# First mixer: the output gate's four projection tiles leave the middle of the attention loop; two stand at its end, two in the recurrence's first two chunks

## What is computed

```python
def even_mixer(h, w_in, w_out, sinks, conv_w, conv_b, i_bias, f_bias, ml_norm):
    p = h @ w_in
    q_a, k_a, v_a, qk_m, v_m, o_m, i_m, f_m = split_cols(p, ...)
    ...
    y_att = sliding_window_sink_attention(q, k, v, sinks)        # 8 query heads of 64, window 128
    ...
    hm = mlstm_chunkwise(q_m, k_m, v_m, log_i, log_f)            # 4 heads, 4 chunks of 128 tokens
    hm = head_layernorm(hm, ML_NORM_EPS).reshape(bsz, T, ML_V_W) * ml_norm.astype(F32)
    y_ml = (hm * jax.nn.sigmoid(o_m.astype(F32))).astype(h.dtype)
    return jnp.concatenate([y_att, y_ml], axis=-1) @ w_out
```

## Time and profile before

| | |
|---|---|
| device time, median of 3 runs | 1441.8 us (1441.53 to 1442.5) |
| the profiled execution | 1446.55 us |
| its span | 1444.7 us |
| PE busy | 1355.6 us, 94% of the span |
| DVE, ACT, POOL busy | 587.0, 541.5, 653.6 us (41%, 37%, 45%) |
| matmuls of tiles (24 a tile), mean of one | 400 to 410 ns, overlapping |
| granted PE clock, mean over the span | 0.961 |

### The profile page before, as it was taken

The page is one execution under the profiler, slowest core; times in us unless marked ns, Lnnn a source line. Parts: engine busy times, 40 slices in busy tenths (PEclk is TensorE's granted clock), DMA queues, the critical chain, the costliest instruction groups (busy, mean ns, idle before and its releaser), DMA issues.

```text
span 1444.7 us, 17744 instructions
## 1 busy us (share of the span) xinstructions
PE 1355.6 (94%) x6427; PEld 1089.8 (75%) x6427; DVE 587.0 (41%) x966; ACT 541.5 (37%) x883; POOL 653.6 (45%) x801
## 2 busy tenths in 40 slices
PE   5999967999999999999899997998799999999998
PEld 4777646788888888886578776888678888888886
DVE  4537575421211212345599376355442122121233
ACT  4346643441322323337444425332334132241332
POOL 5653213564555645553345321211265555455562
PEclk9999978999999999999799988999999999999999
DMA  8322101323323333232122210000033233332321
GB/s 268 88 76 65 50 1 29 103 88 93 98 88 100 89 97 92 87 102 59 44 73 73 59 59 15 1 2 1 29 92 98 88 96 94 89 100 87 102 88 59
DMA packets 202131, 109.13 MB, mean 76 GB/s; under 512 B 4570, under 2 KB 199376, under 8 KB 201936
## 3 DMA queue, kind: packets, MB, share of 16 engines
q1 hardware_dynamic: 201648, 108.16, 25.8%
q0 software_dynamic: 416, 0.07, 0.0%
HBM read 106.11 MB, written 2.10 MB: 75 GB/s over the span
## 4 chain that ended last, share of the span: by engine, by line
PE 75%; DVE 6%; ACT 3%; issue 2%; POOL 0%; DVEq 0%; ACTq 0%; POOLq 0%
PE ps L825 21%; PE ps L826 21%; PE ps L827 21%; PE ps L812 2%; PE ps L1192 1%; DVE late L2397 1%; PE ps L1206 1%; PE ps L1119 1%; PE ps L1245 1%; PE ps L1217 1%; PE ps L1080 0%; PE ps L1260 0%; PE ps L1258 0%; PE ps L1235 0%; ACT arena L1582 0%
## 5 line engine op out<-in xcount | busy, mean ns | idle before, releaser
L747 POOL TENSOR_TENSOR w_lo<-raw_w,w_hi 128x256 fp32r<-128x256 f32 x760 | 618.2, 845 | 639.3 <-ACT w_hi L1311 639.3
L1311 ACT ACTIVATE w_hi<-raw_w 128x1024 fp32r<-128x1024 f32 x190 | 201.2, 1059 | 594.5 <-PE ps L827 447.7
L825 PE MATMUL ps<-hn_hi,w_hi 128*128 128x512 f32 x880 | 360.8, 410 | 3.4 <-POOL w_lo L747 2.5
L826 PE MATMUL ps<-hn_lo,w_hi 128*128 128x512 f32 x880 | 352.8, 401 | 0.0
L827 PE MATMUL ps<-hn_hi,w_lo 128*128 128x512 f32 x880 | 352.4, 400 | 0.0
L825 PE MATMUL ps<-hid_hi,w_hi 128*128 128x512 f32 x640 | 254.2, 397 | 1.1 <-DVE hid_lo L1795 1.1
L826 PE MATMUL ps<-hid_lo,w_hi 128*128 128x512 f32 x640 | 253.8, 397 | 0.0
L827 PE MATMUL ps<-hid_hi,w_lo 128*128 128x512 f32 x640 | 253.7, 396 | 0.0
L825 PEld LDWEIGHTS ps<-hn_hi,w_hi 128*128 128x128 f32 x880 | 168.4, 191 | 53.4 <-issue 11.3
L826 PEld LDWEIGHTS ps<-hn_lo,w_hi 128*128 128x128 f32 x880 | 168.4, 191 | 42.4 <-issue 3.1
L827 PEld LDWEIGHTS ps<-hn_hi,w_lo 128*128 128x128 f32 x880 | 168.2, 191 | 41.2
(11 more groups left out here) (363 smaller groups left out, 1339.4 us busy)
## 6 DMA issues: line engine op xcount, KB each, us to landing
raw_w<-in_w_up SPq DMA_DIRECT2D x64, 512.0 KB, 4.0
raw_w<-in_w_down SPq DMA_DIRECT2D x64, 512.0 KB, 3.6
raw_w<-in_o_w_in SPq DMA_DIRECT2D x27, 512.0 KB, 3.8
raw_w<-in_e_w_in SPq DMA_DIRECT2D x19, 512.0 KB, 3.7
raw_w<-in_e_w_out SPq DMA_DIRECT2D x8, 512.0 KB, 4.0
raw_w<-in_o_w_out SPq DMA_DIRECT2D x8, 512.0 KB, 3.5
rwkv_raw<-in_x SPq DMA_DIRECT2D x4, 512.0 KB, 8.3
out<-arena SPq DMA_DIRECT2D x8, 256.0 KB, 2.9
```

The lines of the kernel that those rows point to most:

```text
L747: nc.gpsimd.tensor_tensor(w_lo[:, n % CUT, ks], raw_w[:, n % RING, ks], w_hi[:, n % CUT, ks].bitcast(F32), ALU.subtract).then_inc(w_cut, 1)
L825: mm(o, a_hi, b_hi, start=(k == 0), stop=False)
L826: mm(o, a_hi, b_lo, start=False, stop=False)
L1311: A(w_hi[:, n % CUT], raw_w[:, n % RING], ACT.Copy).then_inc(w_high, 1)
```

## The change

It replaces the rule "tile 11+u in step u" by two tables. Steps 0 to 3 keep the v tiles; steps 4, 5 and 6 have none; o0 stands in step 7 and o1 in step 9; o2 and o3 stand in chunks 0 and 1, between the scores and the local state, and are turned one chunk later. ACT drains o2 and o3 there, into a new buffer, and takes the Sigmoid at the start of chunk 2, between the roots, so one more table is loaded. `w_ml` gets other places in memory.

```diff
+SLOT_BESIDE = {0: 11, 1: 12, 2: 13, 3: 14, 7: 15, 9: 16}
+SLOT_IN_CHUNK = {0: 17, 1: 18}
...
     for u in range(8 + 3):
-        if u < 8:
-            yield "slot", 11 + u
+        if u in SLOT_BESIDE:
+            yield "slot", SLOT_BESIDE[u]
         if u == 0:
             yield "rope", 3
-        if 1 <= u < 9:
-            yield "turn", EVEN_SLOTS[10 + u][1][1:]
+        if u - 1 in SLOT_BESIDE:
+            yield "turn", EVEN_SLOTS[SLOT_BESIDE[u - 1]][1][1:]
...
+        o_tile = cut(y_t, 2048, 2, T)
...
-        w_ml = cut(late, 0, 4, 4, P)
+        w_ml = [cut(relu_t.rearrange("p a t -> p (a t)"), n * 512, 4, P) for n in range(2)]
+        w_ml += [cut(arena, 2048 + n * 512, 4, P) for n in range(2)]
...
                         close(ins, "qk_st", n, par)
+                    if n in SLOT_IN_CHUNK:
+                        project_in(0, SLOT_IN_CHUNK[n])
+                    if n - 1 in SLOT_IN_CHUNK:
+                        key = EVEN_SLOTS[SLOT_IN_CHUNK[n - 1]][1]
+                        drained(pe, *key)
+                        turn(key[1:], [o_tile[:, n - 1, t * P:(t + 1) * P] for t in range(NT)])
...
-            for j in range(4):
-                drained(act, "o", j)
-            A(o_gate, o_gate, ACT.Sigmoid).then_inc(S["o_sig"], 1)
...
             for n in range(NT):
+                if n in SLOT_IN_CHUNK:
+                    drain(o_tile[:, n, :], *EVEN_SLOTS[SLOT_IN_CHUNK[n]][1])
+                    cut_next()
+                if n - 1 in SLOT_IN_CHUNK:
+                    drain_gate(EVEN_SLOTS[SLOT_IN_CHUNK[n - 1]][1][1:])
+                if n == 2:
+                    for j in range(4):
+                        drained(act, "o", j)
+                    A(o_gate, o_gate, ACT.Sigmoid).then_inc(S["o_sig"], 1)
                 for a in range(2):
```

More of the change, by code:

```diff
@@ L1512, in _ @@
                     for j in range(4):
-                        ins = A(w_ml[:, u, j, :], mtmp[:, u % 2, j * P:(j + 1) * P], ACT.Exp, bias=gg[:, u, j:j + 1])
+                        ins = A(w_ml[u][:, j, :], mtmp[:, u % 2, j * P:(j + 1) * P], ACT.Exp, bias=gg[:, u, j:j + 1])
                     ins.then_inc(S["n_keep"], 1)
@@ L2054, in ml_out @@
                     j = 4 * n + hh
-                    ins = V.tensor_scalar(w_ml[:, n, hh, :], w_ml[:, n, hh, :], mv[:, j, 0:1], mv[:, j, 1:2],
+                    ins = V.tensor_scalar(w_ml[n][:, hh, :], w_ml[n][:, hh, :], mv[:, j, 0:1], mv[:, j, 1:2],
                                           ALU.subtract, ALU.mult)
@@ L2124, in ml_combine @@
                 for hh in range(4):
-                    ins = V.tensor_scalar(w_ml[:, n, hh, :], nn[:, hh // 2, hh % 2, 0:P], dn[:, n % 2, hh:hh + 1], None,
+                    ins = V.tensor_scalar(w_ml[n][:, hh, :], nn[:, hh // 2, hh % 2, 0:P], dn[:, n % 2, hh:hh + 1], None,
                                           ALU.mult)
@@ L2129, in ml_combine @@
                 for hh in range(4):
-                    ins = V.bn_stats(st6[:, hh, :], w_ml[:, n, hh, :])
+                    ins = V.bn_stats(st6[:, hh, :], w_ml[n][:, hh, :])
                 link(ins)
```

12 lines of the change are left out of this document (9 added, 3 removed).

## The result

| | before | changed |
|---|---|---|
| median of 7 runs | 1442.5 us | 1453.06 us |
| lowest, highest | 1441.53, 1448.77 | 1444.53, 1454.32 |
| ratio, 95% interval | | 1.0043 [1.0023, 1.0062] |
| profiled execution, span | 1446.55, 1444.7 | 1452.59, 1450.8 |
| transposes of k | 184.07 | 180.16 |

The changed kernel is slower: 0.43%, some 6.2 us (3.3 to 8.9). The medians lie further apart than the ratio says, 10.6 us, since both kernels' times spread over 7 us or more. The sign is clear of the noise in both; the size is known only to lie between 3.3 and 12.6.

A forecast was written before the change was run, and what follows sets the result against it. PE bounds the kernel as a whole and the attention loop, DVE the recurrence. -5.5 + 4.4 + 3.7 + 1.7 = +4.3 on 1441.8 gives 1446.1 us; range 1440.4 to 1449.4, the forecast's own 1443.7 to 1448.3.

The forecast's parts named there:

- Term 1: Attention loop: two tiles and turns leave PE, new waits for DVE's probabilities take part back; it ends 5.55 earlier, -5.5 us.
- term 4: Attention loop: PE's clock falls to 1.2 GHz after the second new wait, at 148.5; +1.7 us (0 to 2.6).
- first wait: Attention loop: PE newly waits some 3 us for the probabilities of step 3.
- second wait: Attention loop: PE newly waits some 3.4 us for the probabilities of step 4, until 148.48.
- Term 2: Entry of the recurrence, transposes of k to first combine: 19.0 us with two tiles instead of 14.62, +4.4 us.
- Term 3: Rest of the recurrence: POOL's gain (2.8) and low parts (0.9) delay DVE's instructions; +3.7 us (0 to 6.8).
- The rule of the Trainium skill: DVE instructions with two SBUF inputs, or in a two-port mode, and GpSimd block each other fully; term 3 up to 6.8.
- rival (d): Recurrence: meetings with DVE cost whole POOL instructions; +7.4 us, 1449.2 us, chance 10%.
- (a): Entry of the recurrence: tiles vanish in its waits, hidden under DVE's time; 1436.3 us, chance 8%.
- (b): Recurrence: POOL's instructions miss DVE's; 1440.7 us with the clock staying, 1442.4 with its fall, chance 12%.
- (c): Attention loop: the clock does not fall, POOL's meetings as forecast; +2.6 us, 1444.4 us, chance 20%.
- Costed at nothing: ACT's extra table load (1.28) and drains, the weights' DMAs and w_ml's new places: no cost; 3.2 if ACT's cover went.

The follow-up runs named there:

- e2: Changed kernel with POOL's low part of the output projection's second tile moved behind the gate's multiplications; ratio 1.0059 to the kernel before.
- e3: Changed kernel with the loop's two gate tiles in steps 4 and 6 instead of 7 and 9; ratio 1.0006 to the kernel before.
- e4_one: Changed kernel with one gate tile in the recurrence (chunk 0) instead of two, the others in steps 4, 5 and 8; ratio 0.9976 to the kernel before.
- e1: Changed kernel without POOL's four multiplications of the gate by the norm's gain, signals kept; ratio 1.0026 to the kernel before.
- e6: Changed kernel with all gate tiles back in steps 4 to 7; late Sigmoid, late gain and weights' places stay; ratio 1.0034 to the kernel before.
- e12: e4_one with Sigmoid and gain split by gate tile, POOL's last two multiplications waiting for places where DVE reads PSUM; ratio 0.9951 to the kernel before.
- e5: e4_one with Sigmoid and gain split by gate tile, three POOL multiplications ahead of the low part, one behind; ratio 0.9976 to the kernel before.

## Why the prediction was right

The forecast was +4.3 us and slower. Measured were +6.2 (3.3 to 8.9) and, with the same kernel again, +9.4 (6.2 to 12.6), which is above the +7.6 where the forecast's range ended; the median of the changed kernel, 1453.06, is above that range too (it ended at 1449.4). At the transposes of y_ml, where all its terms end, it was +4.16 in the first pair of traces and +3.51 in the second. So the sum held up to there, and what it left out is what lies behind. Term by term, in the first pair:

- **Term 1, the loop, -5.5, and term 4, the clock, +1.7:** together -3.8, measured -3.9 (184.07 to 180.16). The first wait was 2.86 (3.0 forecast). The second was 1.80, where the prediction says 3.4 and its own times give 4.1 (from 140.14, with turns and output 2.65, a row 0.46 and a score 1.14, to 148.48). It was shorter since PE came to it later (its transposes and outputs behind the first wait took 1.54 and 3.17 at the low clock instead of 1.09 and 1.88) and DVE was half a microsecond ahead of my sum; the slip doesn't enter the term, which goes by DVE's times. The first gate tile ended at 157.22 (157.60 forecast). The fall that counts was not where I put it, behind the second wait, but behind the third, 2.22 us long, which I had inside the 6.10 us from step 7's score to the next probabilities and not named as a wait. Its price, 1.73, shows in e2's trace, where it did not happen; I had 1.7. The first fall cost nothing, as the next wait took it up. So the size of term 4 came true by luck: its reason, that a wait longer than the earlier ones of 1.78 and 2.79 brings a fall, doesn't hold in these traces. A wait of 2.22 brought one in three traces out of four, and one of 3.30 in e3 brought none.
- **Term 2, the entry, +4.4:** measured 18.46 - 14.62 = +3.8. The sum of PE's work held (19.0 forecast); local state and numerator took 1.05 and 1.06 at the full clock, where I had put 1.26 from a row at a mixed one. e4_one adds what the sum implied and I had not drawn from it: one tile would have been free.
- **Term 3, POOL beside DVE, +3.7:** measured 31.95 - 27.72 = +4.2, of which 1.2 in the first combine (0.9 forecast) and 3.0 in the second (2.8). e2 shows the first and e1 and e6 the second. The mechanism and the count of the second combine were right, the equal size of 0.70 by luck: four POOL instructions met three short instructions and L2151, which took 0.22, 1.02, 1.03 and 0.74 more. In the first combine the low part met three instructions, not two, for 0.23, 0.48 and 0.49 more. In these rows each stretched instruction of DVE starts while one of POOL's runs and ends within 0.05 us of its end (the first of L2151's four within 0.1), and as DVE's instructions depend on each other, each is caught by the next of POOL's.
- **The rule of the Trainium skill** ("SBUF — State Buffer", "Who interferes with whom") agrees with the traces: 1.19 us for an instruction of 0.17 that ends with POOL's of 1.27 is blocking, not sharing; the two of 1.19 in the changed kernel have both inputs in SBUF; and e12's instruction at 198.68, with one of its inputs in PSUM, and the reciprocal, with a single one, were not slowed. Two inputs in SBUF are not the whole of it: the TENSOR_SCALAR instructions, with one data input in SBUF, were slowed as well (L2145 0.17 to 1.05 in e4, L2118 1.18 to 3.47 in e5). That would be the other case of this page of the Trainium skill, a two-port mode; no view here names the mode. The upper case, rival (d), +7.4, did not come: of POOL's 4.95 us, 0.9 lay before the second combine, and the rest also covers the time that DVE's instructions take by themselves.
- **The rivals.** (a), the tiles vanish in the waits, is refuted for two tiles and true for one (e4_one). (b), POOL misses, by the rows above. (c), no fall of the clock, was half of e2's trace: the fall that costs did not come there, the first one did. It can happen in single executions.
- **Costed at nothing.** ACT's extra table load and the weights' DMAs show in none of the waits. Something did show that had no term, the granted clock at the start of the output's tiles: in windows of 2 us it was back (0.89) from 230 to 232 before and only from 236 on (1.00, with 0.54 from 234 to 236) in the changed kernel, some 5 us later where the y_ml transposes are 4.16 later, so somewhat more of the output ran at half speed; the table above has that stretch 0.6 us longer. I had no term for it, and beyond y_ml none for the 1.9 us by which the rest was longer in this pair of traces (1220.2 against 1218.3), 1.3 of them in the second mixer.

The prediction took the size of a meeting (term 3) from the one meeting that it saw in the trace of the kernel before, and says that there was one. There was a larger one in the same trace, on the last scaling (four take 1.11 alone and 2.14 beside POOL's gate product):

```profile
222.21 1.11 DVE L2055 TENSOR_SCALAR late<-late,small 128x128 f32<-128x128 f32 x4
...
223.45 2.14 DVE L2055 TENSOR_SCALAR late<-late,small 128x128 f32<-128x128 f32 x4
```

```profile
223.47 1.27 POOL L766 TENSOR_TENSOR arena<-arena,late 128x512 f32<-128x512 f32 x1 [4.37 <-DVE late L2055]
```

Its 1.03 is what two of the four instructions then lost (1.02 and 1.03).

## What to carry to other kernels

Before a piece of work is moved into a gap, compare the gap's length with the piece: here one tile of 5.6 us filled 2.8 us of waiting and the lost clock and cost nothing, and the second cost 4.1. Take work evenly out of a loop that PE bounds; three bare steps in a row turned a PE-bound loop into one that waits. And list what else moves with it: the largest cost was a POOL instruction that only came later because its input did, and fell on a chain of short DVE instructions; placed beside DVE instructions that read PSUM it cost 0.3.

## What the runs showed of the hardware that was not expected

- A wait of 2.22 us (at 163.75) was followed by a stretch at the low clock in both traces of the changed kernel and in e1's, and not in e2's, where it was as long and the program ahead of it the same: whether a given wait lowers the clock differs between executions. Length alone doesn't tell either: 2.86 us brought a fall, 1.80 none, and 3.30 in e3 (in front of 166.57, clock 1.00 until 198) none.
- In the part behind the first mixer the same program takes 6 us more or less (it is 1214.8 to 1220.8 us long), more than most of the effects studied here. Some 5 us of that lie in the 275 to 280 us with the second mixer, where the clock of one place was 0.91 in one trace and 0.70 in another; that the clock makes all of it is not shown. Distances between landmarks repeat where whole times do not (first combine to y_ml 31.95 and 31.96 in the two traces of the changed kernel, 27.72 and 27.74 in those of the kernel before).
- DVE's short dependent instructions can lose nearly a whole POOL instruction each (0.17 to 1.19 us), so four POOL multiplications of 1.27 us cost 3.0 in one place and 0.3 for two in another.
